# Turning attention probabilities on VectorE in 32x32 blocks instead of on TensorE in 128x128 blocks

## What is computed

```python
h = rmsnorm(x, ln_gain)
proj = h @ w_in                                   # 2048 x 5376
q_a, k_a, v_a, g_a, b_c, c_c, x_c, g_c, q_m, g_m = split(proj)
o_a = swa_sink_attention(q_a, k_a, v_a, ...)      # 16 heads of 64, 2 kv heads, chunks of 64 queries, 128 keys
o_c = short_gated_conv(b_c, c_c, x_c, conv_w)     # 3 taps
o_m = memory_cross_attention(q_m, mem_h, ...)     # 4 heads of 128, 256 memory tokens
mixed = concat([silu(g_a) * o_a, silu(g_c) * o_c, silu(g_m) * o_m])
x = x + mixed @ w_out
```

## Time and profile before

| | |
|---|---|
| median of 3 runs | 2856.2 us (2855.91 to 2856.42) |
| profiled execution, its own time | 2856.42 us |
| its span, first to last instruction | 2854.6 us |
| mean granted TensorE clock | 0.996 of full speed |
| PE matmuls | 2795.2 us busy, 98% of the span |
| DVE | 1253.0 us, 44% |
| ACT | 1046.3 us, 37% |
| POOL | 1289.7 us, 45% |

### The profile page before, as it was taken

How to read it: one execution, slowest core, us unless ns; L and a number is a source line. 1 busy time by engine, 2 the same in 40 slices (tenths; PEclk the granted TensorE clock), 3 DMA queues, 4 the chain that set the end, 5 groups by cost and what they waited for, 6 DMA issues and landing times.

```text
span 2854.6 us, 37501 instructions
## 1 busy us (share of the span) xinstructions
PE 2795.2 (98%) x13243; PEld 2312.0 (81%) x13243; DVE 1253.0 (44%) x2323; ACT 1046.3 (37%) x2157; POOL 1289.7 (45%) x552
## 2 busy tenths in 40 slices
PE   6999999999999999999999999999999999999999
PEld 4888887888888888788888888788888888878887
DVE  5334464333524446514534346532534344643335
ACT  6333434333323343524332343433332334343333
POOL 4445543444444544344445454344444454434444
PEclk9999999999999999999999999999999999999999
DMA  6322222244532222234443222223453222222354
GB/s 211 116 91 74 86 92 74 90 131 163 167 98 82 82 82 90 81 96 155 163 143 97 71 89 89 76 92 112 151 176 117 89 74 89 89 75 95 126 166 143
DMA packets 160518, 312.65 MB, mean 110 GB/s; under 512 B 11558, under 2 KB 21876, under 8 KB 157556
## 3 DMA queue, kind: packets, MB, share of 16 engines
q1 hardware_dynamic: 139348, 258.30, 28.6%
q10 hardware_dynamic: 21024, 52.44, 5.5%
HBM read 293.13 MB, written 17.56 MB: 109 GB/s over the span
## 4 chain that ended last, share of the span: by engine, by line
issue 57%; POOL 39%; PE 1%; SPq 1%; POOLq 1%; DMA 0%; DVE 0%; ACT 0%; ACTq 0%
POOL w_lo L415 36%; POOL q_scale L421 2%; POOL early L429 1%; SPq L347 1%; POOLq L414 0%; DMA raw<-in_w_mem_kv 0%; POOL x_scale L421 0%; PE acc L1115 0%; PE acc L1117 0%; PE acc L1116 0%; POOL k_scale L421 0%; ACT w_hi L483 0%; SPq L349 0%; PE ps_t L1168 0%; POOLq L460 0%
## 5 line engine op out<-in xcount | busy, mean ns | idle before, releaser
L415 POOL TENSOR_TENSOR w_lo<-raw,w_hi 128x1024 fp32r<-128x1024 f32 x482 | 1181.5, 2451 | 1531.9 <-ACT w_hi L483 1531.9
L483 ACT ACTIVATE w_hi<-raw 128x1024 fp32r<-128x1024 f32 x482 | 510.4, 1059 | 1434.6 <-PE acc L1117 1425.4
L1115 PE MATMUL acc<-h_hi,w_hi 128*128 128x512 f32 x1792 | 708.1, 395 | 0.0
L1116 PE MATMUL acc<-h_lo,w_hi 128*128 128x512 f32 x1792 | 699.5, 390 | 0.0
L1117 PE MATMUL acc<-h_hi,w_lo 128*128 128x512 f32 x1792 | 699.5, 390 | 0.0
L1115 PE MATMUL acc<-w_hi,mix_hi 128*128 128x512 f32 x1088 | 427.4, 393 | 17.5 <-DVE stage L1100 9.4
L1116 PE MATMUL acc<-w_lo,mix_hi 128*128 128x512 f32 x1088 | 424.3, 390 | 0.0
L1117 PE MATMUL acc<-w_hi,mix_lo 128*128 128x512 f32 x1088 | 424.2, 390 | 0.0
L1115 PEld LDWEIGHTS acc<-h_hi,w_hi 128*128 128x128 f32 x1792 | 337.4, 188 | 77.3 <-POOL w_lo L415 0.9
L1117 PEld LDWEIGHTS acc<-h_hi,w_lo 128*128 128x128 f32 x1792 | 337.3, 188 | 71.5
L1116 PEld LDWEIGHTS acc<-h_lo,w_hi 128*128 128x128 f32 x1792 | 337.5, 188 | 67.8
(11 more groups left out here) (152 smaller groups left out, 2153.5 us busy)
## 6 DMA issues: line engine op xcount, KB each, us to landing
raw<-in_w_in SPq DMA_DIRECT2D x336, 512.0 KB, 3.4
raw<-in_w_out SPq DMA_DIRECT2D x130, 512.0 KB, 3.6
xt<-in_x ACTq DMA_DIRECT2D x16, 1024.0 KB, 6.5
stage<-in_x ACTq DMA_DIRECT2D x64, 256.0 KB, 5.5
out<-stage ACTq DMA_DIRECT2D x64, 256.0 KB, 2.9
raw<-in_w_mem_kv SPq DMA_DIRECT2D x16, 512.0 KB, 8.2
ungated<-in_x SPq DMA_DIRECT2D x2, 1024.0 KB, 14.0
early<-in_x SPq DMA_DIRECT2D x2, 1024.0 KB, 10.7
```

Of the source, the lines that this page charges most:

```text
L415: nc.gpsimd.tensor_tensor(w_lo[:, slot_mod % 2, :], raw[:, slot_mod, :], w_hi[:, slot_mod % 2, :].bitcast(F32), ALU.subtract).then_inc(lo_ ...
L483: nc.scalar.activation(w_hi[:, slot_mod % 2, :], raw[:, slot_mod, :], ACT.Copy).then_inc(hi_ready, 1)
L1115: nc.tensor.matmul(dst, st[0], mv[0], start=first, stop=False)
L1116: nc.tensor.matmul(dst, st[0], mv[1], start=False, stop=False)
```

## The change

The transposes of the probabilities leave PE. DVE makes them, with 16 instructions per unit, each of which transposes four 32x32 blocks of one strip of `probs` (32 partitions, 4 x 32 columns) straight into `probs_t`, in SBUF. ACT's copy of units 0 to 7 is gone, and `pt_hi` and `pt_lo` are made from `probs_t` in SBUF instead of from `ps_t` in PSUM. The transposes of unit u stand in DVE's list directly behind its softmax for units 0 to 7, and one slot later for the others, behind that slot's `attention_sum`.

```diff
-TURN_AT = {s + 2: u for s, u in SCORES_AT.items()}
-SPLIT_AT = {s + 2: u for s, u in SCORES_AT.items()}
+TURN_AT = {s + (u >= 8): u for s, u in SCORES_AT.items()}
+SPLIT_AT = {s + 2: u for s, u in SCORES_AT.items() if u >= 8}
 VALUES_AT = {s + 3: u for s, u in SCORES_AT.items()}
...
                 act.wait_ge(turned, U + 3)
                 act.wait_ge(valued, U + 1)
-                if u < 8:
-                    nc.scalar.activation(probs_t[:, u % 2, :, :].rearrange("p a q -> p (a q)"),
-                                         ps_t[:, :], ACT.Copy).then_inc(mem_turned, 1)
-                else:
-                    nc.scalar.activation(pt_hi[:, :], ps_t[:, :], ACT.Copy).then_inc(pt_high, 1)
+                nc.scalar.activation(pt_hi[:, :], probs_t[:, u % 2, :, :].rearrange("p a q -> p (a q)"),
+                                     ACT.Copy).then_inc(pt_high, 1)
...
-                nc.vector.tensor_tensor(pt_lo[:, :], ps_t[:, :],
+                nc.vector.tensor_tensor(pt_lo[:, :],
+                                        probs_t[:, u % 2, :, :].rearrange("p a q -> p (a q)"),
                                         pt_hi[:, :].bitcast(F32), ALU.subtract).then_inc(probs_t_ready, 1)
...
+            def turn_probs(g, u):
+                dve.wait_ge(probs_ready, g * UNITS + u + 1)
+                if u >= 2:
+                    dve.wait_ge(valued, g * UNITS + u)
+                pb = probs[:, u % 2, :].rearrange("p (b k) -> p b k", b=4)
+                for i in range(4):
+                    for j in range(4):
+                        last = nc.vector.transpose(
+                            probs_t[32 * j:32 * j + 32, u % 2, :, 32 * i:32 * i + 32],
+                            pb[32 * i:32 * i + 32, :, 32 * j:32 * j + 32])
+                last.then_inc(turned, 1)
...
-                    if s in SPLIT_AT and SPLIT_AT[s] >= 8:
+                    if s in SPLIT_AT:
                         probs_low(g, SPLIT_AT[s])
+                    if s in TURN_AT and TURN_AT[s] >= 8:
+                        turn_probs(g, TURN_AT[s])
                     if s in SCORES_AT:
                         softmax(g, SCORES_AT[s])
+                    if s in TURN_AT and TURN_AT[s] < 8:
+                        turn_probs(g, TURN_AT[s])
...
                 if u < 8:
-                    pe.wait_ge(mem_turned, g * 8 + u + 1)
+                    pe.wait_ge(turned, U + 3)
                 else:
                     pe.wait_ge(probs_t_ready, g * 16 + u - 6)
...
-            def turn_probs(g, u):
-                pe.wait_ge(probs_ready, g * UNITS + u + 1)
-                if u == 0:
-                    pe.wait_ge(k_ready, g * 2 + 2)
-                elif u <= 8:
-                    pe.wait_ge(mem_turned, g * 8 + u)
-                else:
-                    pe.wait_ge(probs_t_ready, g * 16 + u - 7)
-                for p in range(4):
-                    last = nc.tensor.transpose(ps_t[:, P * p:P * p + P],
-                                               probs[:, u % 2, P * p:P * p + P], ident[:, :])
-                last.then_inc(turned, 1)
```

More of the change, by code:

```diff
@@ L266, in program @@
         probs_t_ready = sem("probs_t_ready")
-        mem_turned = sem("mem_turned")
         valued = sem("valued")
@@ L1284, in _ @@
                             values(g, VALUES_AT[at])
-                        if at in TURN_AT:
-                            turn_probs(g, TURN_AT[at])
                         if at in SCORES_AT:
```

## The result

| | before | changed | ratio (95% interval) |
|---|---|---|---|
| median of 4 runs | 2856.31 us | 2934.96 us (2932.59 to 2936.57) | 1.0273 (1.026 to 1.0288) |
| span of the profiled execution | 2854.6 us | 2932.4 us | +77.8 us |
| mean granted TensorE clock | 0.996 | 0.984 | |

What follows compares the result with a forecast made beforehand. PE bounds the kernel (98% of the span), but the DVE-ACT loop becomes slower than its slots. Five stretches sum to +20.1 us per group, 80.4 in four, plus 1.6 for clock: 82 on 2856.4 makes 2938 us, range 2890 to 2975.

Steps and rivals of the forecast that it cites:

- PE's saving: Four transposes per unit leave PE's list: 0.44 us per unit, 10.6 per group, 42.2 in four.
- The price of a block transpose: On DVE, 16 block transposes of 128 columns per unit: 0.315 us each, 5.04 us per unit.
- The bounds of 0.235 and 0.446: Limits for one block transpose: 0.235 us if neighbours overlap (2872 us in all), 0.446 as the 256-column form.
- The rival of hidden transposes: DVE keeps ahead everywhere, so PE's saving arrives whole: 2814 us; anything faster than before had 6 in 100.
- The loop: DVE and ACT handing on to each other in a banded unit: 12.75 us, against 12.15 for PE's two slots.
- Stretch 1: Memory units up to the scores of unit 8: wait 4.5 at `scores`(7), clock 1.6, less PE's saving; +2.6 us per group.
- Stretches 2 to 4: Unit 8 to X (slot 44), X to B (slot 52), B to `values`(19): +7.0, +2.7 and +1.8 us per group.
- Stretch 5: From `values`(19) to slot 68, with slot 67 at a low clock: 52.5 us against 46.5 before, +6.0 per group.
- `pt_lo` meets `w_lo`: DVE's `pt_lo`, now reading SBUF, waits for POOL's `w_lo` and ends at best 0.55 us after it; 0 to 1.8 us.
- the rival without meetings: Lateness moves `pt_lo` past `w_lo`'s end, so they don't meet: +15 us per group, 2916 us; 17 in 100.
- The rival in which the clock stays high: PE's clock stays high after the waits: +18.7 us per group, 2931 us; 12 in 100.
- The profile after: DVE at 61%; PE waits at `scores`(7), (23), slots 44, 52, 60; banded waits for `w_lo` and `pt_lo` below 3 us.

Runs made afterwards that it cites:

- 60 of the 96 turns: Against the changed kernel: fifteen units on DVE directly behind their softmax, the nine others transposed on PE; 2829.48 us, ratio 0.9903 to before.
- the run one slot sooner: Against the changed kernel: banded units' transposes directly behind their own softmax, ahead of the sum of the unit before; 2911.76 us, ratio 1.019 to before.
- The run without them: Against the changed kernel: `pt_lo` takes its first operand from PSUM bank `ps_t` (stale values), not from `probs_t` in SBUF; 2913.93 us, ratio 1.0203 to before.

## Why the prediction was right

**PE's saving** (42.2 us). 26.9 us for 60 of the 96 turns, where nothing new waits, is 0.45 each: right as a price. In the changed kernel most of it can't be collected, as the run with the old transposes put back shows.

**The price of a block transpose** (0.315 apart, 5.04 per unit). 5.05 for 16 and 0.303 for one: right. The bounds of 0.235 and 0.446 were both far away. The prediction takes 390 ns for TensorE's transpose from the Trainium skill, page "VectorE: DVE Perf Modes", section "The three transpose paths", which gives it for bf16; these blocks are float32, and they start 0.11 us apart. The rival of hidden transposes falls. The run with half of them, 2.5 us per unit, came out faster than before but with 26.6 of the 42.2 us. Three quarters make 3.78 us per unit, which is 16 at 0.236: there the prediction's lists gave 2872, and 2863 was measured.

**The loop** (12.75 us). Right in kind, 0.2 too long: 12.53. ACT's `w_hi` starts before the read of the last exponential sum has ended, which my sum of two whole pieces left out. Over PE's 12.15 this is 0.4 per unit and not 0.6. Eleven such loops in a group (six, three and two in stretches 2, 4 and 5) make about 17 us in four groups, an estimate. That is a small part of the 120.9, and the run one slot sooner, which has no overlong loop, fits: it gave back 23. The prediction's sentence that the loop is now the slower one holds; most of its sum, and of the loss, comes from the single places that its stretches list.

**Stretch 1.** The wait at `scores`(7) was 2.69 and not 4.5. I took the means of slot 21 at 3.3 us from those of slot 31, which had met `w_lo`: the small second instruction took 1.1 us there, and 0.18 here. The means of slot 21 itself stood in the trace before with 2.27 and 0.18 us, so I took the wrong row. Two more waits of 0.3 were in neither sum.

**Stretches 2 to 4.** Right within 1.2 us each, in every group. In stretch 2 errors of both signs met: a shorter loop and shorter means, but the scaling of the queries took 4.5 where I had 2.3. It met `w_lo`, and I had counted such meetings for `pt_lo` alone.

**Stretch 5** came to 3.6 for 6.0 in the first group only, 7.0 and twice 5.5 in the others (in the 7.0 are the 1.5 us of the clock that had stayed high there before). I had a low clock in slot 67. In the first group the clock fell already after the wait at `scores`(23), PE came later to its next wait, which was 1.81 us, and the clock stayed high in slot 67. In the other three it stayed high after `scores`(23), the next wait was 3.3 us, and the clock fell in slot 67, as forecast. The third group, timeline and then windows:

```profile
1928.10 0.37 PE L1206 MATMUL ps_s<-keys,early 64*128 64x128 f32 x1 [2.82 <-ACT probs L594]
...
1943.28 0.50 PE L1233 MATMUL ps_o<-pt_hi,vals 128*128 128x512 f32 x1 [3.32 <-DVE pt_lo L868]
```

```profile
1928.00:1934.00 6.00, 5.90 (x31) 4.85 (x32) 5.16 (x16) 1.65 (x4) 2.40 (x1) 1.00 0.21 52
1943.00:1948.00 5.00, 4.72 (x14) 3.72 (x15) 4.79 (x17) 0.76 (x2) 2.46 (x1) 0.66 0.60 165
```

**`pt_lo` meets `w_lo`.** I had taken it in at three or four places per group, and the rival without meetings gave 2916. The run without them measured 2914. The meetings are real and worth 21 us.

**The clock.** The mean of 0.984 over 2932 us makes 94 us at half speed, against 23 before. In the changed kernel 20 of PE's 23 waits of 2.7 to 3.9 us in the attention are followed by the lower level. The three that are not are those of 2.82 us at `scores`(23) in the later groups, so the length of a wait alone doesn't decide it. Half of the 71 us more is 35: that much the clock can account for at most, beside the 74.5 of new waits. What it alone cost was not measured, since much of it lies where PE waits again for DVE. The rival in which the clock stays high, 2931, is refuted by these rows and not by the time, which lies between its figure and 2938.

**The profile after.** The waits stand where the prediction put them. The longest for `pt_lo` is 3.6 us and not below 3. DVE's share is 58% and not 61%; the prediction's own figures, 1253 + 480 over 2938, make 59%.

The total is nearer than the parts of the first group, which lost 18.2 us from the keys' turn to the next one; the others lost about 20, with 20.1 forecast, and there the parts are near as well. The later groups lose more by the clock: the low stretch of slot 67 is 0.9 us, a low clock that lasts 6.8 in place of 3.4 us after X's emptying in the third and fourth is 1.4, and the second had kept its clock high before, which is 1.5. Luck lies inside stretches 1 and 2, where errors of both signs met.

## What to carry to other kernels

An engine at 44% can't be given work by its share: ask whether the new work lies inside a loop of hand-overs between engines, add that loop up from the timeline and hold it against the time that the bounding engine has for the same unit. Here 12.5 against 12.15 us used up most of what PE saved on these units (0.38 of 0.44 us each). Then look for the single places where something urgent stands behind the new work, for they cost more: with the loop at 11.4 us the kernel was still 55 us slower than before, and with the nine units taken off that stand ahead of a mean, a bank's emptying, a gate or the narrow end it was 27 us faster. Last, look at where the moved operands lie, since reading SBUF in place of PSUM brought a collision worth 21 us in the kernel where DVE was late.

## What was not expected of the hardware

Small DVE instructions can pay for the meeting with POOL too: the second instruction of the means of slot 31, 128x32 elements, took 1.10 us in the kernel before, where it ended with a `w_lo`, and 0.18 in the changed one. The scaling of 2048 columns took 4.51 in place of 2.28, begun 0.03 us after a `w_lo`. POOL pays as well: the `w_lo` that came during that scaling, at 340.85, took 3.87 us in place of 2.4. The block transposes did not: all 1536 took between 0.292 and 0.311 us, whatever POOL did.
